# Cross attention with scores and weighted values as three fp32r products of parts

## What is computed

```python
def memory_cross_attention(h, mem, w_q, w_k, w_v, w_o):
    q, k, v = h @ w_q, mem @ w_k, mem @ w_v        # 4 heads of 256 features
    p = softmax(q @ k.T / sqrt(256))               # per head, 512 x 256
    return (p @ v) @ w_o
```

## Time and profile before

| | us |
|---|---|
| median of three runs | 2520.03 |
| lowest, highest | 2519.97, 2525.08 |
| the profiled execution | 2524.29 |
| its span in the trace | 2522.5 |

### The profile page before, as it was taken

The page is one execution under the profiler, slowest core; times in us unless marked ns, Lnnn a source line. Parts: engine busy times, 40 slices in busy tenths (PEclk is TensorE's granted clock), DMA queues, the critical chain, the costliest instruction groups (busy, mean ns, idle before and its releaser), DMA issues.

```text
span 2522.5 us, 38409 instructions
## 1 busy us (share of the span) xinstructions
PE 2471.1 (98%) x15181; PEld 2144.2 (85%) x15181; DVE 1699.1 (67%) x3249; ACT 1294.5 (51%) x2558; POOL 404.4 (16%) x476
## 2 busy tenths in 40 slices
PE   7999999999999999999999999999999999999998
PEld 6876677899988978778897999889898887999888
DVE  5476977688863499997774988535635744987533
ACT  4365554367742435564654687424534453677422
POOL 2233342200000156553000100000000100100000
PEclk9999999999999999999999999999999999999999
DMA  9532234434443233223421333332321442333332
GB/s 285 136 93 71 63 101 121 132 99 126 118 126 98 80 101 94 58 67 95 131 84 51 92 111 108 96 96 82 93 76 34 134 126 59 85 111 107 93 99 86
DMA packets 455092, 253.29 MB, mean 100 GB/s; under 512 B 16458, under 2 KB 449310, under 8 KB 454911
## 3 DMA queue, kind: packets, MB, share of 16 engines
q1 hardware_dynamic: 451615, 243.18, 33.7%
q0 software_dynamic: 3152, 7.59, 1.2%
q10 hardware_dynamic: 144, 0.07, 0.0%
HBM read 247.99 MB, written 2.80 MB: 99 GB/s over the span
## 4 chain that ended last, share of the span: by engine, by line
PE 84%; DVE 10%; ACT 3%; issue 2%; DMA 1%; SPq 0%; POOL 0%; DVEq 0%; ACTq 0%; POOLq 0%
PE ps L1134 15%; PE ps L1136 15%; PE ps L1142 15%; PE ps L1199 4%; PE ps L1201 4%; PE ps L1204 4%; PE ps L1049 4%; PE ps L1051 4%; PE ps L1047 4%; PE ps L1375 2%; PE ps L1232 1%; DVE ps L3034 1%; PE ps L1229 1%; PE ps L1227 1%; PE ps L1720 1%
## 5 line engine op out<-in xcount | busy, mean ns | idle before, releaser
L1950 ACT ACTIVATE wh<-w_f 128x512 fp32r<-128x512 f32 (+2 forms) x621 | 351.1, 614 | 337.7 <-PE ps L1142 158.1
L2914 DVE TENSOR_TENSOR w_r<-w_f,wh 128x512 fp32r<-128x512 f32 (+1 forms) x459 | 295.9, 688 | 334.1 <-ACT wh L1950 333.6
L1134 PE MATMUL ps<-XH,wh 128*128 128x512 f32 (+1 forms) x1136 | 458.0, 403 | 4.4 <-ACT wh L1950 3.5
L1136 PE MATMUL ps<-XL,wh 128*128 128x512 f32 (+2 forms) x1016 | 398.0, 392 | 0.2 <-DVE XL L3434 0.2
L1142 PE MATMUL ps<-XH,w_r 128*128 128x512 f32 (+2 forms) x1160 | 309.2, 390 | 1.1 <-DVE w_r L2914 0.8
L1136 PE MATMUL ps<-arena_r,wh 128*128 128x512 f32 (+1 forms) x808 | 297.1, 373 | 0.1
L4213 POOL TENSOR_TENSOR w_r<-w_f,wh 128x256 fp32r<-128x256 f32 (+1 forms) x314 | 236.1, 782 | 352.2 <-ACT wh L1950 352.2
L1134 PEld LDWEIGHTS ps<-XH,wh 128*128 128x128 f32 (+1 forms) x1136 | 211.9, 186 | 69.2 <-issue 16.0
L1142 PEld LDWEIGHTS ps<-XH,w_r 128*128 128x128 f32 (+2 forms) x1160 | 215.5, 186 | 51.2 <-DVE w_r L2914 3.2
L1136 PEld LDWEIGHTS ps<-XL,wh 128*128 128x128 f32 (+2 forms) x1016 | 189.5, 186 | 42.8 <-issue 1.7
L1134 PE MATMUL ps<-arena_r,wh 128*128 128x512 f32 (+1 forms) x568 | 210.6, 379 | 0.8 <-ACT wh L1950 0.8
(11 more groups left out here) (499 smaller groups left out, 5913.4 us busy)
## 6 DMA issues: line engine op xcount, KB each, us to landing
w_f<-in_mlp_w SPq DMA_DIRECT2D x126, 512.0 KB, 4.0
w_f<-in_w_ff SPq DMA_DIRECT2D x63, 512.0 KB, 4.1
w_f<-in_w_in SPq DMA_DIRECT2D x49, 512.0 KB, 3.9
w_f<-in_ada_w SPq DMA_DIRECT2D x35, 512.0 KB, 4.0
w_f<-in_even_w_in SPq DMA_DIRECT2D x35, 512.0 KB, 3.8
w_f<-in_odd_w_in SPq DMA_DIRECT2D x23, 512.0 KB, 3.7
w_f<-in_even_w_out SPq DMA_DIRECT2D x16, 512.0 KB, 3.9
w_f<-in_xa_w_v SPq DMA_DIRECT2D x16, 512.0 KB, 3.3
```

The lines of the kernel that those rows point to most:

```text
L1134: e.matmul(b, hi[:, k, :], xh, start=u.first and k == 0, stop=False)
L1136: e.matmul(b, hi[:, k, :], xl, start=False, stop=False)
L1950: e.activation(high_flat(u)[:, s], flat(u, 0)[:, s], ACT.Copy).then_inc(act.sem, act.up("high", u.n, i))
L2914: e.tensor_tensor(low[:, s], raw_[:, s], high[:, s], ALU.subtract).then_inc(dve.sem, dve.up("low", u.n, i))
```

## The change

Queries, keys, values and softmax weights get high and low parts, and each fp32 product becomes three fp32r products: two per tile become six of 256 columns, four per head twelve of 512 columns.

- ScalarE: the query units are copied to `q_high` instead of `qT`; two new copies each for `keys_high` and `values_high` per stage; the transposes are copied to `pt_high`.
- VectorE: `q_low` from the bank of each query unit, which it frees in ScalarE's place; `weights_low` for each tile two iterations later, from the bank of the transposes, which it frees in ScalarE's place.
- GpSimd: `keys_low` and `values_low`, one subtraction of 128 x 2048 each per stage.
- The areas of keys, values, parts and output parts in SBUF are laid out anew.

```diff
--- before.py
+++ after.py
@@ -88,6 +88,8 @@
 O_SUMS = 16512
 O_PRODUCT = O_SUMS + 8 * S * 2 + HALF_SHIFT
 NEAR = 8
+O_KEYS = 12416
+O_PT_LOW = ARENA - 1024 - 16
 
 ADA_AFTER = {1: 0, 4: 1, 7: 2, 10: 3}
 ADA_SECOND = ADA_LATE + len(ADA_AFTER)
@@ -800,19 +802,28 @@
 
         qT, o = area(0, KC, S)
         ws2, o = area(o, 4, MEM)
-        PT2, o = area(o, 2, 2, S)
-        assert o <= O_XBC
-        kT, o = area(-(-(O_XBC + KC * S) // 16) * 16, KC, MEM)
+        pt_high, o = area(o, 2, 2, S, r=True)
+        pt_low = [area(o, 2, S, r=True)[0], area(O_PT_LOW, 2, S, r=True)[0]]
+        assert o + 2 * S <= O_LEAD - HALF_SHIFT
+        kT, o = area(O_KEYS, KC, MEM)
+        k_low = area(O_KEYS, KC, MEM, r=True)[0]
+        O_VALUES = o
         vv, o = area(o, 2, D)
-        O_MEM = o
+        v_low = area(O_VALUES, 2, D, r=True)[0]
+        O_OUT_LOW = o
+        k_high, o = area(O_OUT_LOW + KC * S, KC, MEM, r=True)
+        v_high, o = area(o, 2, D, r=True)
+        assert o <= O_PT_LOW
+        o = O_MEM = O_OUT_LOW + 112
         mem_high, o = area(o, KC, MEM, r=True)
         mem_low, o = area(o, KC, MEM, r=True)
         mem, o = area(o, 2, D)
         weighed = lambda hd: att4 if hd >= 2 else lin
         out_high = area(0, KC, S, r=True)[0]
-        out_low = area(-(-O_MEM // 32) * 32, KC, S, r=True)[0]
+        out_low = area(O_OUT_LOW, KC, S, r=True)[0]
+        q_high, q_low = out_high, out_low
         xa_ring = [Ring(f"xa {li}", [ws2[:, j, :] for j in range(4)], rings) for li in range(2)]
-        pt_ring = [Ring(f"pt {li}", [PT2[:, j, :, :] for j in range(2)], rings) for li in range(2)]
+        pt_ring = [Ring(f"pt {li}", [(pt_high[:, j, :, :], pt_low[j]) for j in range(2)], rings) for li in range(2)]
 
 
         o = 0
@@ -852,7 +863,8 @@
 
 
         copied = {"aq": aq, "ak": ak, "bq": bq, "iq": iq, "cq": cq, "ck": ck, ("mk", 0): kT, ("mk", 1): kT,
-                  ("xq", 0): qT, ("xq", 1): qT, "oq": q_, "ok": k_}
+                  "oq": q_, "ok": k_}
+        cross_queries = ("xq", 0), ("xq", 1)
 
         TURNED = ("iw", "dt")
 
@@ -1714,11 +1726,14 @@
                 def cross_begin(hd, qt):
                     b, freed = att4.take("x", li, hd, qt)
                     w.wait_ge(*freed)
-                    w.wait_ge(act, ("xq", li), 2 * hd + 1)
-                    w.wait_ge(act, ("mk", li), KC - 1)
+                    w.wait_ge(dve, ("xq", li), 2 * hd + 1)
+                    w.wait_ge(act, "keys high", li)
+                    w.wait_ge(pool, "keys low", li)
                     for j in range(2):
-                        last = e.matmul(b[:, 0:MEM], qT[:, 2 * hd + j, qt * P:(qt + 1) * P], kT[:, 2 * hd + j, :],
-                                        start=j == 0, stop=j == 1)
+                        m, ts = 2 * hd + j, slice(qt * P, (qt + 1) * P)
+                        e.matmul(b[:, 0:MEM], q_high[:, m, ts], k_high[:, m, :], start=j == 0, stop=False)
+                        e.matmul(b[:, 0:MEM], q_high[:, m, ts], k_low[:, m, :], start=False, stop=False)
+                        last = e.matmul(b[:, 0:MEM], q_low[:, m, ts], k_high[:, m, :], start=False, stop=j == 1)
                     last.then_inc(pe.sem, pe.up("x", li, hd, qt))
 
                 def cross_end(hd, qt):
@@ -1732,14 +1747,18 @@
                     xa_ring[li].free(pe, hd, qt)
 
                 def cross_weigh(hd):
-                    pt = pt_ring[li].of(hd)
-                    w.wait_ge(act, "xpt", li, hd, NT - 1)
-                    w.wait_ge(act, "stored", ("mv", li), KC - 1)
+                    high, low = pt_ring[li].of(hd)
+                    w.wait_ge(dve, "xpt", li, hd, NT - 1)
+                    w.wait_ge(act, "values high", li)
+                    w.wait_ge(pool, "values low", li)
                     for m in (2 * hd, 2 * hd + 1):
                         b, freed = weighed(hd).take("xv", li, m)
                         w.wait_ge(*freed)
+                        c = slice(m * P, (m + 1) * P)
                         for kt in range(2):
-                            last = e.matmul(b[:, :], vv[:, kt, m * P:(m + 1) * P], pt[:, kt, :], start=kt == 0, stop=kt == 1)
+                            e.matmul(b[:, :], v_high[:, kt, c], high[:, kt, :], start=kt == 0, stop=False)
+                            e.matmul(b[:, :], v_high[:, kt, c], low[:, kt, :], start=False, stop=False)
+                            last = e.matmul(b[:, :], v_low[:, kt, c], high[:, kt, :], start=False, stop=kt == 1)
                         last.then_inc(pe.sem, pe.up("xv", li, m))
                     pt_ring[li].free(pe, hd)
 
@@ -2100,6 +2119,9 @@
                     w.wait_ge(pe, "unit", u.n)
                     copy(copied[name][:, m, :], b, name, m)
                     lin.free(act, *u.out)
+                elif name in cross_queries:
+                    w.wait_ge(pe, "unit", u.n)
+                    copy(q_high[:, m, :], b, "query high", name[1], m)
                 elif name in TURNED:
                     g, freed = gate_ring.take("turn", name, m)
                     w.wait_ge(*freed)
@@ -2688,6 +2710,17 @@
                         layer_bias(st)(k)
                 return biases
 
+            def keys_high(li):
+                for h in range(2):
+                    ks = slice(h * QUARTER, (h + 1) * QUARTER)
+                    w.wait_ge(act, ("mk", li), KC - 1)
+                    copy(k_high[:, ks, :], kT[:, ks, :], "keys high", li)
+
+            def values_high(li):
+                for t in range(2):
+                    w.wait_ge(act, "stored", ("mv", li), KC - 1)
+                    copy(v_high[:, t, :], vv[:, t, :], "values high", li)
+
             def cross_attention(stage):
                 li = stage - 1
 
@@ -2706,9 +2739,8 @@
                         _, freed = pt_ring[li].take(hd)
                         w.wait_ge(*freed)
                     w.wait_ge(pe, "xt", li, hd, qt)
-                    copy(pt_ring[li].of(hd)[:, :, qt * P:(qt + 1) * P],
+                    copy(pt_ring[li].of(hd)[0][:, :, qt * P:(qt + 1) * P],
                          att4.of("xt", li, hd, qt)[:, 0:MEM].rearrange("p (a b) -> p a b", a=2), "xpt", li, hd, qt)
-                    att4.free(act, "xt", li, hd, qt)
 
                 def cross_high(hd):
                     for m in (2 * hd, 2 * hd + 1):
@@ -2732,10 +2764,13 @@
                 half_norm((stage, 1), plans[(stage, "o"), "tail"], plans[(stage, "ff1"), "lead"], layer_high((stage, 1)))
                 mlp(stage, lambda k: ln_b((stage, 1), k), layer_bias((stage, 1)))
 
-            run((1, "out"))
+            run_steps(plans[1, "out"][:3])
+            keys_high(0)
+            run_steps(plans[1, "out"][3:])
             half_norm((1, 0), plans[(1, "out"), "tail"], plans[(1, "q"), "lead"], layer_high((1, 0)))
             run(((1, "q"), "lead"))
             run((1, "q"))
+            values_high(0)
             cross_attention(1)
             half_norm((1, 2), plans[(1, "ff2"), "tail"], plans["gla", "lead"], layer_high((1, 2)))
 
@@ -2851,7 +2886,9 @@
                 run_steps([u])
                 layer_bias((2, 0))(k)
             flush()
+            keys_high(1)
             run((2, "q"))
+            values_high(1)
             cross_attention(2)
             def token_moments(half):
 
@@ -3062,6 +3099,11 @@
                     w.wait_ge(pe, "unit", u.n)
                     e.scalar_tensor_tensor(out=hT[:, m, :], in0=hT[:, m, :], scalar=ALPHA, in1=b[:, :],
                                            op0=ALU.mult, op1=ALU.add).then_inc(dve.sem, dve.up("yout", m))
+                    lin.free(dve, *u.out)
+                elif name in cross_queries:
+                    w.wait_ge(act, "query high", name[1], m)
+                    e.tensor_tensor(q_low[:, m, :], b[:, :], q_high[:, m, :].bitcast(F32), ALU.subtract).then_inc(
+                        dve.sem, dve.up(name, m))
                     lin.free(dve, *u.out)
                 elif name[0] == "ff1":
                     st = name[1]
@@ -3951,6 +3993,13 @@
                     e.tensor_scalar(row, row, st[:, 3:4], None, ALU.mult).then_inc(dve.sem, dve.up("xp", li, hd, qt))
                     st_ring.free(dve, "x", li, hd, qt)
 
+                def weights_low(hd, qt):
+                    high, low = (a[:, :, qt * P:(qt + 1) * P] for a in pt_ring[li].of(hd))
+                    w.wait_ge(act, "xpt", li, hd, qt)
+                    e.tensor_tensor(low, att4.of("xt", li, hd, qt)[:, 0:MEM].rearrange("p (a b) -> p a b", a=2),
+                                    high.bitcast(F32), ALU.subtract).then_inc(dve.sem, dve.up("xpt", li, hd, qt))
+                    att4.free(dve, "xt", li, hd, qt)
+
                 def cross_low(hd):
                     for m in (2 * hd, 2 * hd + 1):
                         low_part(out_low[:, m, :], weighed(hd).of("xv", li, m)[:, :], out_high[:, m, :], ("o", li), m)
@@ -3958,11 +4007,15 @@
 
                 for i, tile in enumerate(tiles):
```

(18 more changed lines are left out.)

## The result

The changed kernel is slower: 2535.64 us median of 4 runs (2533.57 to 2538.01), against 2522.25 of the kernel before in the same comparison; the ratio is 1.0047, 95% interval 1.003 to 1.0065, that is 8 to 16 us. Forecast were 2530.7 against the 2520.03 known then, +10.7; the measured ratio of 1.0047 makes +11.9.

What follows compares the result with a forecast made beforehand. TensorE, busy 98% of the span, was taken to bound the kernel, so its savings and waits count in full. The terms -10.8 + 11.8 + 6.8 + 2.1 + 0.8 make +10.7 us: 2530.7 against 2520.03, range 2517 to 2538.

Steps and rivals of the forecast that it cites:

- The products: TensorE's score and weighing products in both cross attentions: shorter as fp32r parts, -10.8 us.
- The third rival: Score products don't get shorter, 0.215 us each at equal offsets: +22 us, 2542; chance 0.07.
- After the last query unit: Behind i = 10 in both stages, TensorE waits for VectorE's queue: 5.9 us each, 11.8 in all.
- The start of the first attention: Start of stage 1: values_high and values_low delay tile 0 and what follows; TensorE waits 6.8 us.
- The hold: Tile 0's scaling on VectorE is held until GpSimd's values_low ends, 1313.5 to about 1317.3 in stage 1.
- The start of the second: Start of stage 2: same delay of tile 0, mostly hidden by query units; 2.1 us, 0.7 without it.
- `keys_low`: GpSimd's subtraction in stage 1's last mixer output units delays VectorE splits: 0.8 us (0 to 2); nothing in stage 2.
- The rival without a hold: Tile 0's scaling beside GpSimd only runs slower: the two starts cost 3.0 + 0.7, +5.5 us, 2525.5; chance 0.18.
- the faster one: Two tiles of lead cover VectorE's work after units i = 2, 5, 10: -9.4 us, 2510.6; chance 0.13.

Runs made afterwards that it cites:

- e_full2: e_full with ScalarE's two values copies one query unit earlier in both attentions; 2512.9 us against 2523.53 for the kernel before, ratio 0.9956.
- e_order: Changed kernel with weights_low(i-2) behind the query unit's splits and q_low in VectorE's order instead of ahead of them; ratio 1.0026 to the kernel before.
- e_pieces: Changed kernel with GpSimd's values_low as eight subtractions of 256 columns instead of one of 2048; ratio 1.0024 to the kernel before.
- e_weigh: Changed kernel with only the weighing in parts, scores and their operands as before the change; ratio 1.0034 to the kernel before.
- e_scores: Changed kernel with only the scores in parts, weighing and its operands as before the change; ratio 0.9979 to the kernel before.
- e_early: Changed kernel with values_high and values_low, still one subtraction, moved ahead of the query phase; ratio 1.0040 to the kernel before.
- e_best: Changed kernel with e_shadow, e_early and both GpSimd subtractions in eight pieces of 256 columns; ratio 0.9993 to the kernel before.
- e_full3: e_full2 with weights_low(0) later, in the fourth tile's wait for its exponential; ratio 0.9955 to the kernel before.
- e_both: Changed kernel with the edits of e_order and e_pieces together; ratio 1.0004 to the kernel before.
- e_full: Changed kernel with e_shadow's order, values_low on VectorE at i = 5, first and third weighings later, keys_low in eight pieces; ratio 0.9978 to the kernel before.
- e_full_keys1: e_full with keys_low as one GpSimd subtraction of 2048 columns; ratio 0.9980 to the kernel before.
- e_shadow: Changed kernel with weights_low(i-3) in VectorE's wait for the exponential and cross_low(1) later; ratio 1.0001 to the kernel before.

## Why the prediction was right

The sign, the sum and the mechanism held. What follows counts losses from start to start, and leaves out the 0.6 us in all that the kernel before loses at the same places. That the sum lies so near is in part luck: one cost that no term had, TensorE's clock, is made up for in good part by terms that came out smaller.

- **The products**, -10.8 (the two parts given for it, 5.2 and 5.4, make 10.6): -10.5. Scores give 2.23 in an attention without a wait, not 2.6: the first of a tile's six products takes 0.20 us after the transposes. Scores and weighing give 75.63 - 70.86 = 4.77 in e_full2, whose one wait there still costs 0.46 (scores 1.12 instead of 0.79, the weighing 2.85 instead of 2.72); so 5.2 in each attention, and the weighing 3.0 where 2.7 was forecast. The third rival (no shorter at equal offsets) falls.
- **After the last query unit**, 5.9 twice: 5.8 and 5.7. That it comes from the order on VectorE is shown by e_order. Up to the third weighing 4.5 was forecast, and 4.5 and 4.3 were lost, but the first step was misplaced: I put 1.6 on the output products, for the unit's bank; the trace has 2.4 on scores 12, one step earlier, which need that unit's `q_low` itself, and no idle time before the output products. The third weighing's 2.9 came out as 1.9 in the second attention, and in the first as 0.5 and 1.6 of lower clock in its place. The transposes behind it cost 1.3 against 1.4.
- **The start of the first attention**, 6.8: 8.0. The hold is as read from the earlier trace rows, and the waits stand where they were put: 3.2 up to transposes 2 (3.5 forecast), 2.5 at scores 5 (2.6), 0.7 at the first weighing (0.7). What no term had is TensorE's clock behind them, 1.7 (below).
- **The start of the second**, 2.1: 1.5, at the first weighing. The pieces take 0.9 off that attention, where the hold was forecast at 1.4.
- **`keys_low`**, 0.8: 0.8, and nothing with the pieces; nothing in stage 2, as forecast (678.8 us between the attentions before, 678.7 after).
- The sum of these is +11.3, by the lengths 8.48 + 1.91 + 0.8 = 11.2, against +10.7. The rival without a hold falls by the 4.14 us scaling; the faster one by the 14.6 us of waits. Its condition, that the work fits, could be met by moving it (e_full2).

## What to carry to other kernels

When a product is split into parts, count the subtractions' places before their durations: an in-order engine that stands for another engine's copy holds all that is queued behind it, so put such an instruction behind work that is ready, or into a wait that is there anyway. A long instruction on an engine that shares a lock is priced by what the other engine has due in that time; cut it, or move it to where nothing is due. Compare the stage's own length where the rest of the program varies by as much as the effect.

## What the runs showed that was not expected

TensorE's clock fell to its lower level (1.2 of 2.4 GHz) behind some waits. The windows of the changed kernel's first attention (granted clock is the third figure from the end):

```profile
1313.41:1325.41 12.00, 10.11 (x59) 8.39 (x57) 7.49 (x13) 5.73 (x13) 4.60 (x1) 1.00 0.29 87
1325.41:1332.41 7.00, 4.11 (x13) 3.33 (x14) 5.37 (x16) 3.05 (x9) 0.00 (x0) 0.53 0.01 4
1332.41:1363.41 31.00, 28.34 (x150) 23.91 (x150) 15.79 (x42) 15.79 (x37) 0.00 (x0) 1.00 0.17 51
1363.41:1367.41 4.00, 4.00 (x17) 3.33 (x16) 2.60 (x11) 1.68 (x6) 0.00 (x0) 0.58 0.00 0
```

In the first of the two slow stretches, six score products take 1.44 us (1328.99 to 1330.43) where 0.80 is usual (1341.53 to 1342.33), and the sixteen products that open the unit 4.69 (1330.43 to 1335.12) against 3.66 in the unit before (1315.56 to 1319.22): 1.7 in all. The second cost next to nothing: scores 12 to the third weighing took 7.36, and 7.22 at full clock in e_pieces, where a wait of 1.67 stood in its place. e_weigh's first attention has 0.53 over 7 us too.

Most of the runs have the first stretch. From scores 5 to the end of the unit behind them it is 6.3 us in e_scores, e_early, e_best, e_full2 and e_full3; 7.7 to 7.9 in the changed kernel, e_order, e_pieces, e_both, e_full and e_full_keys1; 8.7 in e_shadow; and with fp32 scores 6.5 before and 8.9 in e_weigh. Less this difference, the first attentions of e_order, e_both, e_full and e_weigh, 0.7 to 2.2 above their ranges, lie in them. Of the 2.6 us that e_full2 gains on e_full there, 1.5 is the clock.

The Trainium skill ("TensorE: Matmul & The Clock Gate", Part 1) says that the array's clock is gated by how busy the engine has been; both stretches follow idle time (1.29 and 2.23 us, and 2.17), which agrees with it. But a like wait does not always bring it: in the second attention 2.17 and 1.62 left the clock at 1.00, while 2.16 before the same scores 12 in e_early was followed by 0.53 (2116 to 2118). Ahead of the first attention, in code that these two kernels share, waits of 2.24 and 0.77 us were followed by full clock in e_both, and of 2.26 and 0.76 by half clock in e_full, which fell back by 2.8 us there (from 1.75 us behind the kernel before to 4.58); the first view is e_both's, the second e_full's:

```profile
1240.00:1248.00 8.00, 7.82 (x34) 6.50 (x35) 3.92 (x7) 2.62 (x5) 0.00 (x0) 1.00 0.00 0
```

```profile
1242.00:1248.00 6.00, 5.97 (x14) 4.71 (x15) 3.77 (x6) 2.49 (x5) 0.00 (x0) 0.50 0.00 0
```

That makes part of the spread between runs of one kernel, and of the profiled difference. Which of two like waits brings it stays open.
